# A hybrid decoder step on Trainium2: the activation region starts at a multiple of 256 bytes of SBUF

## The chip, the core and the metric

The kernel runs on one core of one Trainium2 chip. The core has TensorE (PE: matmuls, and PEld: its weight loads), VectorE (DVE), ScalarE (ACT), GpSimd (POOL), SyncE (SP), which here only issues DMAs, and 16 DMA engines. SBUF is the on-chip memory: 128 partitions, and every tensor has the same address in each. PSUM, in 8 banks, takes what TensorE computes. The metric is the time of one execution on the device in microseconds. The median of three runs of the kernel before is 1775.49 us.

## The reference

One step of a two-layer decoder for 288 tokens: a prompt of 256 and 8 samples of 4. All arithmetic is float32. Each layer has a mixer (a gated delta rule and a convolution module side by side) and a feed-forward part, which is dense in the first layer and has 8 experts, two for each token, in the second:

```python
for layer in range(DEPTH):
    mod = (jax.nn.silu(c) @ w_ada[layer] + b_ada[layer])[:, None, :]
    shift1, scale1, gate1, shift2, scale2, gate2 = jnp.split(mod, N_MOD, axis=-1)
    h = rms_norm(x, g_norm1[layer]) * (1 + scale1) + shift1
    proj = h @ w_in[layer]
    ...
    o_a, buf_a, s_a = gdn_mixer(qkv_in, z, b_raw, a_raw, ...)
    o_b, buf_b = conformer_conv(glu_u, glu_g, ...)
    x = x + gate1 * (jnp.concatenate([o_a, o_b], axis=-1) @ w_out[layer])
    h = rms_norm(x, g_norm2[layer]) * (1 + scale2) + shift2
    if layer % 2 == 0:
        f = swiglu(h, w_ff_gate[idx], w_ff_up[idx], w_ff_down[idx])
    else:
        f = moe_swiglu(h, w_router[idx], b_router[idx], w_exp_gate[idx], w_exp_up[idx], w_exp_down[idx])
    x = x + gate2 * f
return rms_norm(x, g_final), new_s, new_conv, new_conf
```

The model width is 1024, the dense hidden width 2816, that of an expert 3584. The outputs are the normed tokens and the new states of the delta rule and of the two convolutions.

## The kernel before

**Weights.** The host cuts all weights into units of 128 x 2048 float32 (1024 KB). SyncE loads 455 of them, one after the other, into a ring of six buffers, `raw`. Where precision asks for it, ScalarE rounds a unit to a high part in a ring of three, `whi` (line 666), and VectorE subtracts to get the low part in `wlo` (line 1040). TensorE then multiplies three times: high by high, high by low, low by high. These lines are 1681 to 1683 for tiles of weights against 288 tokens, and 2222 to 2224 in the expert stage.

**Stages.** First the modulation from the conditioning vectors (line 1692) and the first norm. Then, for each layer, the input projection, the mixer and the output projection, and the feed-forward part. In the dense layer the activations are the moving operand: eight tiles of `h_hi` and `h_lo` for the up projection (a loop of six units a turn), 22 tiles of `act_hi` and `act_lo` for the down projection. In the expert stage the roles are reversed: rows of gathered tokens (`ht_hi`, `ht_lo`) and of hidden values (`at_hi`, `at_lo`) are the stationary operand, and 512 columns of `whi` or `wlo` move. It is a loop over the experts' 42 units each, with the gather for the next expert and the scatter of the last one (`facc`, line 1599) put in between.

**SBUF.** The program lays its tensors out by hand. One big tensor, the arena, begins at 4224 and ends at 229304. Inside it `keep` hands out places in order: the three rings (12 buffers of 8192 bytes, the first at 4224), then `x`, the parameters, the constants and small tiles that live throughout. Where these end, at 139648, begins a region of 89088 bytes in which all else has its place as a fixed distance from the variable `r0`. Tiles of different stages share bytes there. The addresses of the rings are 128 above a multiple of 256, all of them, since 8192 is a multiple and 4224 = 16 x 256 + 128. So is 139648 = 545 x 256 + 128.

**What lies in the region**, with the distance from one tile to the next:

- 1152 bytes (288 tokens), so that tiles are in turn at 128 and 0 above a multiple of 256: `h_hi`, `h_lo`, `hf`, `sq`, `qkv`, `zs`, `yc`, `oall`, `act_hi`, `act_lo`, `facc`.
- a multiple of 256, so that all tiles lie as the region does: `ht_hi`, `ht_lo`, `at_hi`, `at_lo`, `ye_hi`, `ye_lo`, `pe_sel`, the 512-byte and 2048-byte blocks of the delta rule, the states `sst` (rows of 4096 bytes).
- neither: `qpad` (1260 bytes) and `cpad` (2232 bytes), the padded inputs of the two convolutions. VectorE reads them with a start that moves by 4 bytes for each tap (lines 1130 and 1110).

GpSimd issues the DMAs of the states and the pads: `sst<-gdn_in`, `gdns_out<-sst`, `qpad<-qst_in`, `cpad<-cst_in` and the outputs `qst_out` and `cst_out`. SyncE issues `y_out<-hf` at the end. No other DMA touches the region but that of the conditioning vectors at the start.

The order of work on every engine is written out in the program, and semaphores join the engines. No address has a part in it.

## Time and profile before

| | |
|---|---|
| median of 3 runs | 1775.49 us (1774.6 to 1776.69) |
| the profiled execution | 1778.42 us, its span 1776.6 us |
| TensorE busy | 1730.5 us, 97% |
| VectorE busy | 1370.4 us, 77% |
| ScalarE busy | 1034.5 us, 58% |
| GpSimd busy | 81.3 us, 5% |
| mean granted clock of TensorE | 0.976 of full speed |
| mean DMA rate | 281 GB/s |

The span goes from the first to the last instruction of the program; the execution's time is 1.8 us more. Busy times of engines overlap each other, so they say which engine has room, not which one sets the end. For that the profile follows a chain back from the last instruction, at each step to what released it. A matmul's recorded duration (390 ns for 512 columns) is longer than the distance of one from the next (227 ns), because they are pipelined: the starts of neighbours give the rate.

### The profile page before, as it was taken

What the parts mean: (1) busy time and instruction counts of PE and PEld (TensorE: products, weight loads), DVE (VectorE), ACT (ScalarE), POOL (GpSimd) and SP (SyncE); (2) the same over time, 40 slices, a digit from 0 to 9 for tenths busy, and PEclk for the clock granted to TensorE, in tenths of its full rate; (3) what the DMA queues carried; (4) which work ended last, traced back from release to release, by engine and by line L of the source; (5) the groups of instructions that cost most, each with busy time, mean ns of one, the idle gap of its engine ahead of it and who ended that gap; (6) DMA issues with size and microseconds to landing.
All of it is one profiled execution on the core that took longest, in us unless ns stands there. A gap on an engine that the chain in (4) does not pass through costs nothing.

```text
span 1776.6 us, 25456 instructions
## 1 busy us (share of the span) xinstructions
PE 1730.5 (97%) x9464; PEld 1448.7 (82%) x9464; DVE 1370.4 (77%) x1627; ACT 1034.5 (58%) x989; POOL 81.3 (5%) x97
## 2 busy tenths in 40 slices
PE   6999999999999999889999999999999999999997
PEld 3878977999978798668888888888888888888886
DVE  2698564554438984678898898898898988988998
ACT  3246423443333544157777777777777777777775
POOL 0112100000011220000000000000000000000000
PEclk8999899999999998989999999999999999999999
DMA  9686019444466520459999999999999999999996
GB/s 384 268 312 233 2 71 363 164 165 166 167 250 270 209 96 7 143 210 358 347 371 339 363 359 355 358 370 337 373 355 347 363 355 352 359 355 362 362 366 260
DMA packets 70186, 499.49 MB, mean 281 GB/s; under 512 B 7968, under 2 KB 8096, under 8 KB 11072
## 3 DMA queue, kind: packets, MB, share of 16 engines
q1 hardware_dynamic: 66528, 481.16, 71.2%
q0 software_dynamic: 3552, 16.87, 2.5%
q8 instruction: 72, 1.18, 0.3%
q14 instruction: 34, 0.28, 0.0%
HBM read 485.95 MB, written 12.05 MB: 280 GB/s over the span
## 4 chain that ended last, share of the span: by engine, by line
PE 91%; DVE 5%; DMA 2%; issue 1%; ACT 0%; SPq 0%; DVEq 0%
PE ps L2222 17%; PE ps L2223 17%; PE ps L2224 17%; PE ps L1681 5%; PE ps L1683 5%; PE ps L1682 5%; PE ps L2026 4%; PE ps L1863 3%; DMA raw<-units 2%; PE ps L1692 2%; PE ps L2199 1%; PE ps L2166 1%; PE ps L1702 1%; DVE yc L1110 1%; PE ps L1772 1%; PE ps L1787 1%
## 5 line engine op out<-in xcount | busy, mean ns | idle before, releaser
L1040 DVE TENSOR_TENSOR wlo<-raw,whi 128x2048 fp32r<-128x2048 f32 x384 | 876.8, 2292 | 180.3 <-ACT whi L666 180.3
L666 ACT ACTIVATE whi<-raw 128x2048 fp32r<-128x2048 f32 x384 | 735.9, 1918 | 251.5 <-PE ps L2224 203.1
L2222 PE MATMUL ps<-whi,ht_hi 128*128 128x512 f32 x896 | 355.5, 397 | 1.7 <-DVE ht_lo L1585 1.7
L2223 PE MATMUL ps<-wlo,ht_hi 128*128 128x512 f32 x896 | 349.4, 390 | 0.0
L2224 PE MATMUL ps<-whi,ht_lo 128*128 128x512 f32 x896 | 349.3, 390 | 0.0
L2224 PEld LDWEIGHTS ps<-whi,ht_lo 128*128 128x128 f32 x896 | 168.2, 188 | 35.9
L2222 PEld LDWEIGHTS ps<-whi,ht_hi 128*128 128x128 f32 x896 | 168.3, 188 | 34.9 <-issue 1.9
L2223 PEld LDWEIGHTS ps<-wlo,ht_hi 128*128 128x128 f32 x896 | 168.5, 188 | 31.4
L2222 PE MATMUL ps<-whi,at_hi 128*128 128x512 f32 x448 | 175.1, 391 | 0.0
L2223 PE MATMUL ps<-wlo,at_hi 128*128 128x512 f32 x448 | 174.4, 389 | 0.0
L2224 PE MATMUL ps<-whi,at_lo 128*128 128x512 f32 x448 | 174.4, 389 | 0.0
L1681 PE MATMUL ps<-h_hi,whi 128*128 128x288 f32 x560 | 167.6, 299 | 0.0
L1682 PE MATMUL ps<-h_lo,whi 128*128 128x288 f32 x560 | 165.5, 295 | 0.0
L1683 PE MATMUL ps<-h_hi,wlo 128*128 128x288 f32 x560 | 164.9, 294 | 0.0
L1681 PEld LDWEIGHTS ps<-h_hi,whi 128*128 128x128 f32 x560 | 105.3, 188 | 10.1 <-issue 8.4
L1683 PEld LDWEIGHTS ps<-h_hi,wlo 128*128 128x128 f32 x560 | 105.7, 189 | 0.0
L1682 PEld LDWEIGHTS ps<-h_lo,whi 128*128 128x128 f32 x560 | 105.5, 188 | 0.1
L1110 DVE SCALAR_TENSOR_TENSOR yc<-cpad,par,yc 128x256 f32<-128x256 f32 x240 | 104.2, 506 | 0.0
L2224 PEld LDWEIGHTS ps<-whi,at_lo 128*128 128x128 f32 x448 | 84.1, 188 | 17.6
L2222 PEld LDWEIGHTS ps<-whi,at_hi 128*128 128x128 f32 x448 | 84.1, 188 | 16.7
L2223 PEld LDWEIGHTS ps<-wlo,at_hi 128*128 128x128 f32 x448 | 84.1, 188 | 16.6
L2026 PE MATMUL ps<-hf,raw 128*128 128x288 f32 x352 | 91.7, 421 | 2.8 <-DVE hf L1090 2.8
(347 smaller groups left out, 2031.4 us busy)
## 6 DMA issues: line engine op xcount, KB each, us to landing
raw<-units SPq DMA_DIRECT2D x455, 1024.0 KB, 5.9
sst<-gdn_in POOLq DMA_DIRECT2D x8, 512.0 KB, 6.1
gdns_out<-sst POOLq DMA_DIRECT2D x8, 512.0 KB, 6.6
qst_out<-qpad POOLq DMA_DIRECT2D x2, 1890.0 KB, 9.0
cst_out<-cpad POOLq DMA_DIRECT2D x2, 1116.0 KB, 11.1
x<-x_in SPq DMA_DIRECT2D x1, 1152.0 KB, 9.1
y_out<-hf SPq DMA_DIRECT2D x2, 576.0 KB, 2.9
con<-const_in SPq DMA_DIRECT2D x1, 1141.5 KB, 18.8
```

The lines of the kernel that those rows point to most:

```text
L666: act.activation(whi[s % NSPLIT][:, :], raw[u % NRAW][:, :], ACT.Copy).then_inc(hi_split, 1)
L1040: dve.tensor_tensor(wlo[s % NSPLIT][:, :], raw[unit_of(s) % NRAW][:, :], whi[s % NSPLIT][:, :].bitcast(F32), ALU.subtract).then_inc(lo_spl ...
L1110: dve.scalar_tensor_tensor(y, cp3[:, c, j:j + TP], w, y, ALU.mult, ALU.add).then_inc(tap_prompt, 1)
L1681: mm(out, w_hi, x_hi, start=start, stop=False)
L1682: mm(out, w_hi, x_lo, start=False, stop=False)
L1683: return mm(out, w_lo, x_hi, start=False, stop=stop)
L1692: last = mm(ps[32 * k:32 * k + 32, bank, :], cst3[:, 4 * half + k], raw[u % NRAW][:, k * 512:(k + 1) * 512], start=(half == 0), stop=(half ...
L1863: last = mm(ps[:, bank, 0:T], raw[u % NRAW][:, w], part, start=(k == 0), stop=(k == 3))
L2026: last = mm(ps[:, bank, 0:T], raw[u % NRAW][:, w], hf3[:, k], start=(k == 0), stop=(k == KD - 1))
L2222: mm(ps[:, bank, :], a_hi[:, a], whi[u % NSPLIT][:, w], start=(first and i == 0), stop=False)
L2223: mm(ps[:, bank, :], a_hi[:, a], wlo[u % NSPLIT][:, w], start=False, stop=False)
L2224: last = mm(ps[:, bank, :], a_lo[:, a], whi[u % NSPLIT][:, w], start=False, stop=(end and i == 3))
```

## The change

The start of the region is rounded up to the next multiple of 256:

```diff
@@ -286,7 +286,7 @@
         posT = keep("posT", T)
         npass_i = keep("npass_i", 1, I32)
 
-        r0 = cursor[0]
+        r0 = (cursor[0] + 255) // 256 * 256
         h_hi = at("h_hi", r0, KD * T, F32R)
         h_lo = at("h_lo", r0 + 9216, KD * T, F32R)
         hf = at("hf", r0 + 18432, KD * T)
```

In the built program `r0` goes from 139648 to 139776 = 546 x 256. The 97 tensors of the region lie 128 bytes higher, and the other ones, with the rings at 128 above a multiple, stay. The region then ends at 228864, 440 bytes below the arena's end. On all five engines the instructions are the same ones in the same order.

The lines of the layout that the sections below speak of:

Of the kernel before, what the change touches and what calls it, by code (L numbers as in the profile page):

```python
# [254 lines left out]
def program(nc, units, x_in, c_in, par_in, const_in, gdn_in, qst_in, cst_in,  # L255
            y_out, gdnp_out, gdns_out, qst_out, cst_out):
    ctx = ExitStack()
    with ctx:
# [3 lines left out]
        cursor = [base]  # L262

        def at(name, offset, cols, dt=F32):
            return nc.alloc_sbuf_tensor_at(name, [P, cols], dt, offset=offset)
# [20 lines left out]
        posT = keep("posT", T)  # L286
        npass_i = keep("npass_i", 1, I32)

        r0 = cursor[0]
        h_hi = at("h_hi", r0, KD * T, F32R)  # L290
        h_lo = at("h_lo", r0 + 9216, KD * T, F32R)
        hf = at("hf", r0 + 18432, KD * T)
# [2072 lines left out]
```

## Rows read from the trace of the kernel before

**Rows 1.** The page: busy times (share of the span), and the chain by engine.

```profile
PE 1730.5 (97%) x9464; PEld 1448.7 (82%) x9464; DVE 1370.4 (77%) x1627; ACT 1034.5 (58%) x989; POOL 81.3 (5%) x97
...
PE 91%; DVE 5%; DMA 2%; issue 1%; ACT 0%; SPq 0%; DVEq 0%
```

**Rows 2.** By stretch: length, busy PE, PEld, DVE, ACT, POOL; clock, DMA share, GB/s.

```profile
298.00:411.00 113.00, 113.00 (x849) 113.00 (x849) 56.50 (x54) 53.27 (x58) 0.00 (x0) 1.00 0.50 179
830.00:1570.00 740.00, 740.00 (x3414) 613.66 (x3413) 658.57 (x443) 542.28 (x372) 0.00 (x0) 1.00 0.94 357
```

**Rows 3.** Waits, 765 to 1756 us: waiter, waited for, us in total, times, longest.

```profile
ACT whi L666 <- PE ps L2224: 202.3, 255, 2.2
```

**Rows 4.** VectorE alone in a stretch: length, busy (instructions), clock, DMA share, GB/s.

```profile
567.50:613.80 46.30, 44.54 (x95) 1.00 0.57 223
```

**Rows 5.** The chain in order of time, two pieces: start, length, what.

```profile
270.94 11.56 DMA raw<-units
...
510.42 6.71 DMA raw<-units
```

**Rows 6.** TensorE in the up loop: start, length, instruction.

```profile
329.82 0.30 PE L1681 MATMUL ps<-h_hi,whi 128*128 128x288 f32 x1
...
330.22 0.29 PE L1681 MATMUL ps<-h_hi,whi 128*128 128x288 f32 x1
...
330.62 0.30 PE L1681 MATMUL ps<-h_hi,whi 128*128 128x288 f32 x1
```

**Rows 7.** TensorE in the down projection.

```profile
440.46 0.30 PE L1681 MATMUL ps<-act_hi,whi 128*128 128x288 f32 x1
...
440.86 0.29 PE L1681 MATMUL ps<-act_hi,whi 128*128 128x288 f32 x1
```

**Rows 8.** TensorE in the expert stage; eight matmuls stand between these.

```profile
911.16 0.39 PE L2223 MATMUL ps<-wlo,ht_hi 128*128 128x512 f32 x1
...
913.20 0.39 PE L2223 MATMUL ps<-wlo,ht_hi 128*128 128x512 f32 x1
```

**Rows 9.** The page's groups of instructions: count, busy us, mean ns, idle before.

```profile
L1040 DVE TENSOR_TENSOR wlo<-raw,whi 128x2048 fp32r<-128x2048 f32 x384 | 876.8, 2292 | 180.3 <-ACT whi L666 180.3
...
L2222 PEld LDWEIGHTS ps<-whi,ht_hi 128*128 128x128 f32 x896 | 168.3, 188 | 34.9 <-issue 1.9
...
L2222 PEld LDWEIGHTS ps<-whi,at_hi 128*128 128x128 f32 x448 | 84.1, 188 | 16.7
```

**Rows 10.** Weight loads of `hf` at line 2003: one stretch, then all.

```profile
64.42 2.76 PEld L2003 LDWEIGHTS ps<-par,hf 128*128 128x128 f32 x24
...
L2003 PEld LDWEIGHTS ps<-par,hf x96: 106/192/192, 63.5 to 544.6; 128*128 128x128 f32 x64, 128*32 128x32 f32 x32
```

**Rows 11.** Lines with tiles 1152 bytes apart: minimum, median, maximum in ns.

```profile
L1599 DVE TENSOR_TENSOR facc<-ps,facc x56: 448/449/451, 907.0 to 1689.5; 128x288 f32<-128x288 f32 x56
...
L1468 DVE TENSOR_TENSOR act_lo<-ctmp,act_hi x22: 457/458/460, 299.2 to 433.5; 128x288 f32 x18, 128x288 fp32r<-128x288 f32 x4
...
L964 ACT ACTIVATE act_hi<-ctmp x22: 442/444/445, 298.6 to 433.0; 128x288 f32 x18, 128x288 fp32r<-128x288 f32 x4
```

**Rows 12.** The taps of the two convolutions, the same view.

```profile
L1110 DVE SCALAR_TENSOR_TENSOR yc<-cpad,par,yc x240: 469/477/1316, 61.0 to 653.7; 128x256 f32<-128x256 f32 x120
...
L1130 DVE SCALAR_TENSOR_TENSOR conv<-qpad,par,conv x36: 529/536/975, 107.2 to 614.7; 128x312 f32<-128x312 f32 x36
```

**Rows 13.** The page's DMA issues: count, KB each, median us to landing.

```profile
sst<-gdn_in POOLq DMA_DIRECT2D x8, 512.0 KB, 6.1
gdns_out<-sst POOLq DMA_DIRECT2D x8, 512.0 KB, 6.6
...
y_out<-hf SPq DMA_DIRECT2D x2, 576.0 KB, 2.9
```

**Rows 14.** GpSimd's DMA issues in order of time.

```profile
263.31 0.55 POOL L642 DMA_DIRECT2D gdns_out<-sst  x1 [26.80 <-DVE sst L1410]
...
506.28 1.06 POOL L605 DMA_DIRECT2D qpad<-qst_in  x1 [0.43 <-issue]
```

## The prediction, made before the changed kernel ran

> **What bounds the kernel now.** I read the page first, then the chain of waits, then stretches of the trace. TensorE is busy for 1730.5 us, 97% of the span of 1776.6, and the chain of work that ended last is 91% TensorE and 5% VectorE, with 2% of DMA [rows 1]. So there are three places in which an address could cost time. Most of it is matmuls back to back: in the expert stage from 830 to 1570 us TensorE is busy all the time at full granted clock, while ScalarE and VectorE have slack and the DMA engines are 94% busy; the loop of the dense layer's up projection (298 to 411 us) is TensorE alone too [rows 2]. The waits of the expert stage agree: ScalarE's `whi` waits 202.3 us for TensorE [rows 3]. VectorE sets the pace in one stretch, the second layer's input projection from 567.5 to 613.8 us, where it is busy for 44.5 us of 46.3 [rows 4]. DMA is waited for on the chain at 270.9 us (11.56 us) and at 510.4 us (6.71 us), both times for weight units; these are the pieces with transfers of the region near them [rows 5].
>
> **The change, part by part.** The change adds no instruction and no wait, and takes none away: all engines' orders are the same. What it does is raise 97 tensors by 128 bytes. Before, the region begins at 139648, which is 128 above a multiple of 256; after, at 139776, which is such a multiple. The rings stay at 128 above one. I call what is left over by 256 the phase. So every term is one question: what does phase 0 instead of 128 cost or save for each kind of access? The trace of before answers most of it, because many tiles of the region are 1152 bytes apart, four and a half times 256: every second one is at phase 0 already, and after the change they only swap.
>
> *Moving operands of TensorE.* In the up loop three matmuls in a row read tile k of `h_hi` and `h_lo`, the next three tile k+1 at the other phase, all against weights at phase 128. The first of three starts at 329.82, 330.22 and 330.62 us: 0.40 us for three at either phase [rows 6]. The same holds for `act_hi` and `act_lo` in the down projection (440.46 to 440.86 us) [rows 7]. The 1680 matmuls on `h_hi` and `h_lo` and the 528 on `act_hi` and `act_lo` swap phases among themselves and cost 0.
>
> *Stationary operands of TensorE.* In the expert stage the region holds the stationary side (`ht_hi`, `at_hi`, their low parts), 3 x 896 + 3 x 448 = 4032 loads at phase 128 before and 0 after [rows 9], and the ring the moving side at 128, unchanged. Nine matmuls go by from 911.16 to 913.20 us, 227 ns each, and a weight load takes 188 ns beside them [rows 8, 9]. A load at phase 0 is seen where the 64 wide loads of `hf` for the gates run: tiles k and k+1 at the two phases, 24 loads in 2.76 us, 115 ns each, with a median and a maximum that are both 192 ns [rows 10]. Were tiles at one phase slower, the two could not be the same. A load can thus follow another after 115 ns, against a spacing of 227 ns in the expert stage: it would have to take 112 ns more to be seen at all. Cost 0; cover 4032 x 227 ns of matmuls.
>
> *ScalarE and VectorE.* The 384 splits of weights read and write rings only and keep their addresses. Operations on tiles that alternate between the phases show one duration: `facc` 448 to 451 ns over 56, `act_lo` 457 to 460 over 22, `act_hi` 442 to 445 over 22 [rows 11]. Where tiles are not a whole number of 128 bytes apart, `yc<-cpad` reads at 31 steps of 4 bytes with 469 to 477 ns from minimum to median, and the taps of `qpad` 529 to 537 [rows 12]: a spread of up to 8 ns, under 2%, whose cause the trace does not show. The maxima of 1316 and 975 ns are far outside of such a spread, and as the order of the engines' work stays, I leave them where they are. GpSimd itself has no part of the chain [rows 1]. If this spread came from addresses, the shift could take or give 8 ns for each of the operations on the path. In the VectorE stretch there are 95 operations [rows 4]: 95 x 8 ns = 0.76 us. Outside of it VectorE holds about 5% of 1776.6 less 44.5 us, some 44 us [rows 1], much of it of the kinds that show one duration; 1% of that is 0.4 us. I take 0 and keep -1.2 and +1.2 us for the range.
>
> *DMA.* Weight units land in the rings and don't change. Into and out of the region go small transfers. `sst<-gdn_in` writes it in 6.1 us and `gdns_out<-sst` reads it in 6.6 us, for the same 512 KB and both at phase 128 [rows 13]. The two differ by 0.5 us, 8%, and that is the most that I can charge to the phase when a transfer reads the region. On the path it could act twice: four `gdns_out` issues, the first at 263.3 us, stand beside the weight units that TensorE waits 11.56 us for [rows 5, 14], at most 8% of 11.56 = 0.9 us; and the last `y_out` of 2.9 us, 0.2 us [rows 13]. Each could be a gain of 0 to 1.1 us together. As a loss I allow the same 8% on writes: `qpad` and `cpad`, issued from 506.3 us on [rows 14], share the DMA engines with the weight units that TensorE awaits for 6.71 us from 510.4 us [rows 5]: 0.5 us. The writes of `sst` are issued well before their values are read and are in no piece of the chain above. Between 0.5 and -1.1 us I take 0, because the two transfers that differ by 8% are both at phase 128, so what sets them apart is not the phase.
>
> The Trainium skill has a rule for this part (DMA: Bandwidth & Descriptors, section How a descriptor splits into AXI transactions): a descriptor that doesn't start at a multiple of 256 bytes begins its first transaction at the boundary below, and the bytes before its start cost beats. By it a row of 4096 bytes at phase 128 costs 132 beats instead of 128, and the reads out of the region would get 3% cheaper: an estimate of 3% of 11.56 + 2.9 us = 0.4 us, and a sum of 1775.1 us. The trace neither confirms nor excludes 3%: the reading transfer is the slower one by 8%, but it also runs beside weight units.
>
> *Sum.* 0 + 0 + 0 + 0, with bounds from -1.2 - 1.1 = -2.3 us to +1.2 + 0.5 = +1.7 us. The profiled execution took 1778.4 us with a span of 1776.6, 1.8 us outside of it; the sum is made against the span and carries over to the median of 1775.5, as the 1.8 us (start and end) touch no address of the region in another way. Predicted: 1775.5 us.
>
> **Rivals.** *Slower: crossed phases.* Before, stationary and moving operands of the expert stage are both at phase 128; after, one is at 0 and the other at 128. If two reads of TensorE at different phases got into each other's way, each of 4032 matmuls would pay. From 0.88 ns each (3.55 us, 0.2% of 1775.5) it shows; at one clock of 2.4 GHz, 0.42 ns, it is 1.7 us and hidden in the noise, at ten, 4.2 ns, it is 16.8 us and gives 1792 us. Against it speaks the up loop, where phases are crossed for every second tile at no cost [rows 6]; for it, only that there the roles are reversed and that this pairing of the expert stage is nowhere in the trace. Chance 6%.
>
> *Faster: the region's accesses were paying for phase 128.* Then the 14 ns between 227 ns and the 213 ns that 512 columns take at 2.4 GHz [rows 8] would be in part a penalty for the load from the region. If 1 ns of the 14 went, 4032 x 1 ns = 4.0 us, 1771.5 us; if all went, 56 us. Against it: the up loop has 133.3 ns for 288 columns, which are 120 ns: the same 13 ns, with its weights from the ring, and at both phases of the activations [rows 6]. The same 13 ns where nothing but the reader's side is exchanged is the mark of a fixed cost of a matmul. The gain from transfers alone (1.1 us) stays below what counts. Chance 6%.
>
> *The change does not do what it says.* The allocation could have put the region at a multiple already, or the rounding could push the last tensor out of the arena. Neither is so: 139648 is 545.5 x 256, and the region's end, 89088 above its start, lies 440 bytes below the limit. The result would be 1775.5 us all the same.
>
> **How the numbers follow.** A measurement of this kernel can tell 0.2%, 3.55 us, from no change; its three runs lie within 2.1 us. No change to be seen: 88% (the last rival is in it), 1775.5 us. Slower by crossed phases 6%, faster 6%. The range that holds 8 in 10 takes the bounds of the sum, -2.3 and +1.7 us, and 1.2 us of spread of the median on either side: 1772.0 to 1778.4, rounded to 1772.0 to 1778.5 us. It leaves both 6% out.
>
> **What would show it.** In the profile after, the starts of three matmuls in the up loop stay 0.40 us apart, and those of the expert stage 0.227 us; a step wrong there would be the whole result. The busy time of `wlo`, 876.8 us, stays within 1 us [rows 9]. `yc<-cpad` keeps its median of 477 ns; if it moves by several ns, the spread did come from addresses. `gdns_out<-sst` at 6.1 instead of 6.6 us would say that reads out of the region paid for their phase. The prediction is wrong if any matmul group's mean spacing changes by a ns, or if TensorE gets new waits of several us.

## The result: 1.1% slower, and all of it in the expert stage

The changed kernel takes 1793.14 us, the median of four runs (1790.23 to 1799.02). The kernel before took 1774.60, 1776.69 and 1775.49 us beside it; a fourth run of it took 1931.77 us, 9% more, which counts as a slow run, and all comparisons go by fast ones. The ratio of the two is 1.0113, with a 95% interval from 1.0085 to 1.014; the medians differ by 17.7 us, where no change was predicted. The profiled execution of the changed kernel took 1793.16 us with a span of 1791.4.

The page of the changed kernel, busy times, the chain by engine, and the groups that answer to [rows 1, 3, 9] (busy us, mean ns, idle before):

```profile
PE 1744.7 (97%) x9464; PEld 1445.5 (81%) x9464; DVE 1372.5 (77%) x1627; ACT 1033.8 (58%) x989; POOL 76.9 (4%) x97
...
PE 91%; DVE 5%; DMA 2%; issue 1%; ACT 0%; SPq 0%; DVEq 0%
...
L1040 DVE TENSOR_TENSOR wlo<-raw,whi 128x2048 fp32r<-128x2048 f32 x384 | 878.2, 2291 | 206.1 <-ACT whi L666 205.8
L666 ACT ACTIVATE whi<-raw 128x2048 fp32r<-128x2048 f32 x384 | 735.5, 1917 | 275.7 <-PE ps L2224 218.3
```

TensorE is busy for 14.2 us more with the same 9464 matmuls. VectorE and ScalarE do the same work in the same time; what grew is what they wait. In the expert stage ScalarE's `whi` waits for TensorE for 218.3 us instead of 202.3 [rows 3]. The chain has the same shares as before. So this is no new wait and no new bound: the engine that was the bound has become slower.

The same stretches as in [rows 2], in the changed kernel (length; busy PE, PEld, DVE, ACT, POOL with their numbers of instructions; clock, DMA share, GB/s):

```profile
830.00:1570.00 740.00, 740.00 (x3341) 601.45 (x3340) 646.97 (x431) 531.19 (x364) 0.00 (x0) 1.00 0.92 349
298.00:411.00 113.00, 113.00 (x849) 113.00 (x849) 57.12 (x53) 52.83 (x57) 0.00 (x0) 1.00 0.46 165
```

Both stretches are wholly TensorE's, at full granted clock, before and after, so the count in the bracket stands for its rate. In the up loop it is 849 matmuls before and after. In the expert stage it is 3341 instead of 3414: the same 3414 would now take 740 x 3414 / 3341 = 756.2 us, 16.2 us more in three quarters of the stage.

Single matmuls show it too. The changed kernel's expert stage (start, length, instruction):

```profile
911.20 0.39 PE L2223 MATMUL ps<-wlo,ht_hi 128*128 128x512 f32 x1
...
911.67 0.39 PE L2222 MATMUL ps<-whi,ht_hi 128*128 128x512 f32 x1
911.89 0.40 PE L2223 MATMUL ps<-wlo,ht_hi 128*128 128x512 f32 x1
912.13 0.39 PE L2224 MATMUL ps<-whi,ht_lo 128*128 128x512 f32 x1
912.36 0.40 PE L2222 MATMUL ps<-whi,ht_hi 128*128 128x512 f32 x1
...
913.29 0.40 PE L2223 MATMUL ps<-wlo,ht_hi 128*128 128x512 f32 x1
```

Nine intervals from 911.20 to 913.29 us are 232 ns each, against 227 [rows 8]; and they are uneven, 0.22 and 0.24 us in turn. For the whole stage I take from the trace the distance from one start to the next wherever six matmuls of the stage stand in a row: 3327 intervals with a mean of 227.0 ns before, 3332 with 233.3 ns after, mostly as 229 and 237 or 238 in turn. Before, over nine in ten of them are 226 or 227 ns, 226.7 in the mean, and the rest are mostly 231 to 233. At 2.4 GHz, 0.4167 ns a clock, 226.7 ns are 512 + 32 clocks, and 233.3 ns are 512 + 48. So most intervals grew by 16 clocks, 6.7 ns, and the mean by 6.3 ns. I call this mean the expert interval below.

The weight loads of line 2222 on `ht_hi`, an answer on one line of the program (minimum, median, maximum in ns, then the two times), before and after:

```profile
L2222 PEld LDWEIGHTS ps<-whi,ht_hi x896: 186/188/192, 772.7 to 1746.8; 128*128 128x128 f32 x180
```

```profile
L2222 PEld LDWEIGHTS ps<-whi,ht_hi x896: 186/188/192, 766.6 to 1761.2; 128*128 128x128 f32 x180
```

From first to last it is 974.1 us before and 994.6 after, 20.5 us more. Taken from the first to the last matmul of the stage, it is 986.1 and 1006.9 us, 20.8 more. The account closes: 3330 intervals x 6.3 ns = 21.0 us. The other 560 or so from one expert matmul to the next, which stand just behind matmuls of another kind or are above 260 ns, have a mean of 242.6 ns before and 242.3 after; together they take no longer. The load itself has not become longer, 188 ns as before.

The span is 14.8 us longer and not 20.8, because the stage begins earlier: at 772.7 us in the execution profiled before, at 766.6 after. Over the kernels below, but for the one with 256 columns in the up loop, it begins between 762 and 773 us, at any phase. Of the 6.1 us, 4.3 are there already at the first matmul of line 1681, 48.6 us into the span before and 44.3 after. The phase of the region doesn't set that start: two kernels below with the region at 128 have it at 44.6 us (the region by 256) and at 48.5 us (rings at 0). One execution of each kernel is profiled, so how the 17.7 us between the medians are made up is not shown.

### The profile page after: what moved, and what is told of

It is laid out like the page before. It is cut to its first block, busy times and chain, and to the rows that moved or that the text cites. A ratio compares the mean times of both kernels' runs of the same rounds, so it can differ in the third digit from the quotient of the medians.

```text
span 1791.4 us, 25456 instructions
## 1 busy us (share of the span) xinstructions
PE 1744.7 (97%) x9464; PEld 1445.5 (81%) x9464; DVE 1372.5 (77%) x1627; ACT 1033.8 (58%) x989; POOL 76.9 (4%) x97
## 4 chain that ended last, share of the span: by engine, by line
PE 91%; DVE 5%; DMA 2%; issue 1%; ACT 0%; SPq 0%; DVEq 0%
PE ps L2224 17%; PE ps L2222 17%; PE ps L2223 17%; PE ps L1681 5%; PE ps L1683 5%; PE ps L1682 5%; PE ps L2026 4%; PE ps L1863 3%; DMA raw<-units 2%; PE ps L1692 2%; PE ps L2199 1%; PE ps L2166 1%; DVE yc L1110 1%; PE ps L1772 1%; PE ps L1787 1%; PE ps L1785 1%
## 5 line engine op out<-in xcount | busy, mean ns | idle before, releaser
L1040 DVE TENSOR_TENSOR wlo<-raw,whi 128x2048 fp32r<-128x2048 f32 x384 | 878.2, 2291 | 206.1 <-ACT whi L666 205.8
L666 ACT ACTIVATE whi<-raw 128x2048 fp32r<-128x2048 f32 x384 | 735.5, 1917 | 275.7 <-PE ps L2224 218.3
L2224 PE MATMUL ps<-whi,ht_lo 128*128 128x512 f32 x896 | 354.1, 395 | 0.0
L2223 PE MATMUL ps<-wlo,ht_hi 128*128 128x512 f32 x896 | 353.5, 395 | 0.0
```

What stands on the lines that cost most here:

```text
L666: act.activation(whi[s % NSPLIT][:, :], raw[u % NRAW][:, :], ACT.Copy).then_inc(hi_split, 1)
L1040: dve.tensor_tensor(wlo[s % NSPLIT][:, :], raw[unit_of(s) % NRAW][:, :], whi[s % NSPLIT][:, :].bitcast(F32), ALU.subtract).then_inc(lo_spl ...
L2223: mm(ps[:, bank, :], a_hi[:, a], wlo[u % NSPLIT][:, w], start=False, stop=False)
L2224: last = mm(ps[:, bank, :], a_lo[:, a], whi[u % NSPLIT][:, w], start=False, stop=(end and i == 3))
```

## Experiments

Phase, as in the prediction, is an address by 256; the difference is the phase of the region's tile less that of the ring's. All kernels are the kernel before with the edit shown, where nothing else is said. `r0` is where the region begins. Each table's time is the median with the number of its runs; the expert interval and those of the 288-column loops are means over the trace, from start to start.

### Is it the region's phase, or the two phases against each other?

Everything by 128 bytes, rings and region:

```diff
-        base = (nc.sbuf_base + 63) // 64 * 64
+        base = (nc.sbuf_base + 255) // 256 * 256
```

> Rings and region both at a multiple of 256 (phase 0): the arena starts 128 bytes higher than in the kernel before, the region stays directly behind the small tiles. Seen so far: with rings at 128 and region at 128 a matmul of the expert stage follows the last after 226.7 ns, with rings at 128 and region at 0 after 229 and 237.5 ns in turn, 233.3 on average. Theory 1, only the difference of the phases counts: 226.7 ns again, and a time of 1773 to 1778 us. Theory 2, a stationary operand at phase 0 is slow wherever the moving one lies: 233.3 ns and 1790 to 1796 us. The new DMA phase of the weight units: up to 1 us less by either.

The same, and the region another 128 bytes on, so that the rings (and the small tiles between them and the region) are at 0 and the region at 128:

```diff
-        base = (nc.sbuf_base + 63) // 64 * 64
+        base = (nc.sbuf_base + 255) // 256 * 256
...
-        r0 = cursor[0]
+        r0 = cursor[0] + 128
```

> The reverse of the change: rings at phase 0, region at phase 128. Theory 1 (the difference counts): crossed again, 233.3 ns in the expert stage and 1790 to 1796 us. Theory 2 (stationary operand at phase 0): 226.7 ns and 1773 to 1778 us. The up loop, whose stationary operands are now at phase 0: 0.40 us for three matmuls by theory 1, more than 0.40 by theory 2 if it holds for any stationary operand.

The region by 256 bytes, which changes its place but not its phase, and by 64:

```diff
-        r0 = cursor[0]
+        r0 = cursor[0] + 256
```

> Control: rings unchanged, the region 256 bytes higher, so at phase 128 as before. If only the address modulo 256 counts: 226.7 ns, the time of the kernel before within 0.2%, 1773 to 1778 us. If the distance or a larger power of two counts: something else, up to the 1793 us of the change.

> Rings unchanged at 128, the region 64 bytes higher than before, at phase 192: the phases differ by 64. If the cost grows step by step with the difference: about half of the change's, 230 ns and 1784 us. If any difference costs the same: 233.3 ns and 1793 us. If only a difference of 128 costs: 226.7 ns and 1776 us.

| | rings at | region at | time, us | ratio to before, 95% interval | expert interval |
|---|---|---|---|---|---|
| before (19 runs beside them) | 128 | 128 | 1772.30 | | 227.0 ns |
| all by 128 | 0 | 0 | 1772.98 (10) | 1.0006 (0.9987 to 1.0025) | 227.0 ns |
| region by 256 | 128 | 128 | 1772.43 (10) | 0.9989 (0.9969 to 1.0008) | 227.0 ns |
| all but the region by 128 | 0 | 128 | 1794.31 (4) | 1.0124 (1.0089 to 1.0159) | 233.3 ns |
| region by 64 | 128 | 192 | 1793.09 (4) | 1.0114 (1.0079 to 1.0149) | 233.3 ns |

The expert stage between 830 and 1570 us, of the kernel with all at 0, and of the one with all but the region at 0:

```profile
830.00:1570.00 740.00, 740.00 (x3413) 613.30 (x3412) 659.04 (x444) 542.67 (x372) 0.00 (x0) 1.00 0.94 357
```

```profile
830.00:1570.00 740.00, 740.00 (x3342) 601.47 (x3341) 646.83 (x431) 530.61 (x363) 0.00 (x0) 1.00 0.93 349
```

3413 and 3342 matmuls: the first is the kernel before (3414), the second the changed one (3341). So a region at a multiple of 256 is neither good nor bad, and nor is a ring. What counts is that both have the same phase. The row of the region by 256 speaks against a cause in some single place, such as a boundary that a tile comes to lie across.

A rival is that TensorE's reads collide with the accesses of others. The trace of the changed kernel answers it. In the expert stage there are 192 intervals in which VectorE is idle (and idle through the next matmul too), and their mean is 232.9 ns; in 406 ScalarE is idle, 234.2 ns; in 17 no DMA packet is under way, 233.8 ns. The same groups of the kernel before have 226.7 ns each (130, 371 and 13 intervals). So the cost is there when each of the others is silent: it is TensorE's own operands that get into each other's way.

### At which differences?

One run each, the edit being another number added to `r0`:

> Rings unchanged, region 32 bytes higher than before (phases differ by 32). The runs so far: a difference of 0 gives 227.0 ns a matmul in the expert stage, 64 and 128 give 233.3 ns. Theory A, any difference costs the 6.3 ns: 233.3 ns, 1790 to 1796 us. Theory B, the two reads of TensorE collide in pieces of 64 bytes, and a smaller shift leaves them in the same piece for half of the time: 227 to 233 ns, 1773 to 1790 us.

> Region 96 bytes higher (difference 96). Theory A: 233.3 ns in the expert stage. Theory B: between the 233.3 ns of 64 and of 128, so the same. For the loops with 288 columns: 133.3 ns at a difference of 0 and 128, 132.3 ns at 64; at 96 I expect one of these two.

> Region 160 bytes higher, the mirror of 96 (160 = 256 - 96). If only the distance of the phases counts: the numbers of the region at 96. If it matters which of the two is ahead: other numbers. Expert stage 233.3 ns by theory A.

> Region 192 bytes higher, the mirror of 64. If only the distance counts: 233.3 ns in the expert stage and 132.3 ns in the loops with 288 columns, 1793 us. If it matters which is ahead: other numbers.

> Region 224 bytes higher, the mirror of 32, which had 233.3 ns. If the cost falls towards 256 as it did at 192 (229.2 ns): 227 to 229 ns and about the time of the kernel before. If not: 233.3 ns.

| added to `r0` | 0 | 32 | 64 | 96 | 128 (the change) | 160 | 192 | 224 | 256 |
|---|---|---|---|---|---|---|---|---|---|
| expert interval, ns | 227.0 | 233.3 | 233.3 | 234.3 | 233.3 | 233.3 | 229.2 | 233.3 | 227.0 |
| interval of the up loop, ns | 133.3 | 133.3 | 132.2 | 132.2 | 133.3 | 133.3 | 132.2 | 132.2 | 133.3 |
| time, us | | 1799.32 | 1793.09 | 1797.48 | 1793.14 | 1794.66 | 1776.42 | 1792.80 | 1772.43 |

The kernel before ran once beside 32, 96, 160 and 192, with 1772.69 us, and once beside 224, with 1779.27. The expert stage with 192 added:

```profile
830.00:1570.00 740.00, 740.00 (x3385) 609.43 (x3384) 655.25 (x441) 538.04 (x370) 0.00 (x0) 1.00 0.94 354
```

In the expert stage it is a step, not a slope: nearly any difference costs the same, 96 one ns more, and 192 only 2.2 ns. I have no explanation for 192. In the up loop tiles are 1152 bytes apart, so a loop holds two differences, the number added and that plus 128. Values with the same two agree there: 0 with 128, 32 with 160, 64 with 192, 96 with 224.

### Only the expert stage?

All tiles of the expert stage are raised by 128 bytes, and the tiles of all other stages stay. Two of the 17 lines of the edit:

```diff
-        ht_hi = [at(f"ht_hi{i}", r0 + 70656 * i, D, F32R) for i in range(2)]
+        ht_hi = [at(f"ht_hi{i}", r0 + 128 + 70656 * i, D, F32R) for i in range(2)]
...
-        at_hi = [at(f"at_hi{i}", r0 + 16384 + 16128 * i, 512, F32R) for i in range(2)]
+        at_hi = [at(f"at_hi{i}", r0 + 128 + 16384 + 16128 * i, 512, F32R) for i in range(2)]
```

> Only the tiles of the expert stage lie 128 bytes higher, in otherwise the kernel before; the mixers' and the dense layer's tiles stay at their phase. If the change costs its time in the expert stage alone: 233.3 ns there and the change's 1790 to 1796 us. If part of it comes from elsewhere: less, down to 1776 us.

Measured: 1792.70 us (4 runs) beside 1775.67 (7), ratio 1.0122, interval 1.0066 to 1.0178; expert interval 233.3 ns. The stage takes 1007.0 us, as with the full change (1006.9). The same stretch and single matmuls of it:

```profile
830.00:1570.00 740.00, 740.00 (x3341) 601.38 (x3340) 646.91 (x431) 531.25 (x364) 0.00 (x0) 1.00 0.93 349
```

```profile
910.99 0.40 PE L2223 MATMUL ps<-wlo,ht_hi 128*128 128x512 f32 x1
911.23 0.39 PE L2224 MATMUL ps<-whi,ht_lo 128*128 128x512 f32 x1
911.46 0.40 PE L2222 MATMUL ps<-whi,ht_hi 128*128 128x512 f32 x1
```

That is the whole of the change's cost, as far as the runs can tell. The transfers and VectorE's and ScalarE's operations on the rest of the region are where they were in this kernel, so no share of it is seen there.

### Which operand?

Of three matmuls, the first streams `whi` against `ht_hi`, the second `wlo` against `ht_hi`, the third `whi` against `ht_lo`. In one kernel only the low stationary parts go to phase 0 (the tiles around them are moved by multiples of 256 to make room, but `sge` and `ae` by 128); in the other the ring `wlo` does, and with it `x`, the parameters and the small tiles behind it:

```diff
-        ht_lo = [at(f"ht_lo{i}", r0 + 70656 * i + 4096, D, F32R) for i in range(2)]
+        ht_lo = [at(f"ht_lo{i}", r0 + (70656 + 512) * i + 4096 + 128, D, F32R) for i in range(2)]
```

> In the kernel before, only the low parts of the stationary operands of the expert stage (one load in three) go to phase 0; moving operands and the high parts stay at 128. In a row the matmuls are hi with whi, hi with wlo, lo with whi. Theory 1a, a load collides with the matmul that runs while it goes on: the matmul before the low one, on wlo, has the longer interval. Theory 1b, it is the matmul that uses the operand: the low one's own interval grows. If the cost belongs to each crossed pair: on average a third of 6.3 ns, 229.1 ns, 1776 + 8 = 1784 us; if it comes from a change of phase from one load to the next, more than that.

```diff
+        cursor[0] += 128
         wlo = [keep(f"wlo{i}", UNIT, F32R) for i in range(NSPLIT)]
...
-        r0 = cursor[0]
+        r0 = cursor[0] + 128
```

> Kernel before, with the three buffers of wlo (and what is behind them up to the region) 128 bytes higher: of the three matmuls in a row of the expert stage only the middle one has its moving operand at phase 0, all else is at 128. If a matmul pays for its own pair or for the load beside it: only the middle one's interval is longer, 233, and the average 229.1 ns. If the one after it pays too, as in the run with the low parts at phase 0: two of three, 231.3 ns.

| interval that begins with | `whi`, hi | `wlo`, hi | `whi`, lo | time, us (1 run) |
|---|---|---|---|---|
| before | 226.8 | 227.0 | 227.0 | |
| changed | 233.2 | 233.4 | 233.2 | |
| low stationary parts at 0 | 227.5 | 232.4 | 233.8 | 1790.25 |
| `wlo` at 0 | 234.4 | 233.4 | 230.3 | 1795.43 |

The loads of the kernel with the low parts at 0 (start, length, instruction) say what runs beside what:

```profile
911.04 0.19 PEld L2224 LDWEIGHTS ps<-whi,ht_lo 128*128 128x128 f32 x1
```

```profile
911.04 0.40 PE L2223 MATMUL ps<-wlo,ht_hi 128*128 128x512 f32 x1
911.27 0.40 PE L2224 MATMUL ps<-whi,ht_lo 128*128 128x512 f32 x1
```

The weights of the next matmul are loaded while the present one streams. If each interval paid for the pair that runs in it, the low parts at 0 would lengthen only the interval of `wlo`, in which `ht_lo` is loaded. It does, to 232.4 ns; but the next one, in which `ht_hi` at 128 is loaded beside `whi` at 128, is 233.8 ns. With `wlo` at 0 all three are longer. Neither run gave the 229.1 ns of a cost for each crossed pair alone: the mean over the three is 231.3 ns with the low parts at 0 and 232.7 with `wlo` at 0. So one operand out of step costs more than its own interval, and which two of TensorE's accesses collide stays open.

### Does the cost go by columns or by matmuls?

The changed kernel with 480 columns, and with 288, in each matmul of the expert stage; the other 32 or 224 columns of each result are left out of the computation:

```diff
-                                w = slice(i * 512, (i + 1) * 512)
+                                w = slice(i * 512, i * 512 + 480)
```

> The changed kernel with 480 instead of 512 columns in the expert stage's matmuls (32 columns of each weight tile are left out). 480 columns are 7.5 times 256 bytes. Theory: the collision costs 16 clocks for each matmul, whatever its width: 480 + 48 clocks, 220.0 ns. Rival: it goes by how the row ends against 256, as with 288 columns, which are 4.5 times 256 and show no cost: 480 + 32 clocks, 213.3 ns.

> The changed kernel, with 288 of the 512 columns in each matmul of the expert stage (the other 224 columns of each result are left out of the computation). Theory A (a matmul whose moving operand lies in the ring and whose stationary one lies in the region pays about 16 clocks at any width): 288 + 48 clocks, 140.0 ns of a matmul. Theory B (narrow matmuls pay little, whichever operand is where, as the 288-column up loop does): 133.3 ns, the up loop's value. The stage may then wait for its transfers or evictions, so the interval is read inside a run of back-to-back matmuls; the time itself says little, some 1400 to 1500 us.

With 480 columns (1745.39 us, one run), most intervals have one value:

```profile
910.95 0.38 PE L2223 MATMUL ps<-wlo,at_hi 128*128 128x480 f32 x1
...
911.16 0.38 PE L2224 MATMUL ps<-whi,at_lo 128*128 128x480 f32 x1
...
912.90 0.38 PE L2223 MATMUL ps<-wlo,at_hi 128*128 128x480 f32 x1
```

From 910.95 to 912.90 us, nine intervals, they are 217 ns; but three quarters of the stage's intervals are 220 ns, 480 + 48 clocks, and the mean is 219.1 ns. So at 480 columns the usual excess over the columns is the same 48 clocks as at 512, and a row that ends in the middle of 256 bytes doesn't escape the cost. The run can't tell a cost for each matmul from one for each column: 16 x 480 / 512 are 15 clocks. Nor was a kernel with equal phases run at 480.

With 288 columns (1674.17 us, one run, far more than the 1400 to 1500 that I expected; the stage now waits in between, at 911.15 us 0.70 us for VectorE's `facc`) the second theory came true:

```profile
912.37 0.29 PE L2222 MATMUL ps<-whi,ht_hi 128*128 128x288 f32 x1
...
913.57 0.29 PE L2222 MATMUL ps<-whi,ht_hi 128*128 128x288 f32 x1
```

Nine intervals in 1.20 us are 133.3 ns, 288 + 32 clocks, and all of the stage's intervals below 150 ns have a mean of 133.4. That is just what the up loop takes, in which the roles are reversed. So with crossed phases it is the width and not the role of the operands that sets the interval. What equal phases would give in the expert stage at 288 columns was not run.

### Was the up loop a fair comparison?

The prediction read from [rows 6] that crossed phases cost nothing. In the up loop every second tile of `h_hi` and `h_lo` is crossed with the rings. In these two kernels the loop reads only the even tiles (all at phase 128, none crossed), or only the odd ones (all crossed). The other half of the activations is left out of the computation and the first half is used twice, or the reverse:

```diff
-... hi3[:, k], lo3[:, k],
+... hi3[:, k // 2 * 2], lo3[:, k // 2 * 2],
```

> Kernel before, but the up projection's matmuls read the even tiles only (tile 0, 0, 2, 2, ... instead of 0, 1, 2, 3, ...; the same number of matmuls, the products of the odd tiles are wrong), so that moving and stationary operands are all at phase 128. Theory C, tiles in turn at both phases pay on both sides alike, which hid the cost: with equal phases the interval falls from 133.3 ns to 288 + 16 clocks, 126.7 ns, or some other value under 133, and the time by up to 1056 x 6.7 ns = 7 us. Theory D, 288 columns don't pay at all: 133.3 ns.

> The same with the odd tiles only (1, 1, 3, 3, ...), so that moving operands are at phase 0 and stationary ones at 128, crossed throughout. Theory C: more than with the even tiles, 133.3 ns or up to 140. Theory D: 133.3 ns.

The stretch from 298 to 411 us, all TensorE, of the kernel with the even tiles, and of that with the odd ones:

```profile
298.00:411.00 113.00, 113.00 (x861) 113.00 (x859) 57.40 (x54) 53.27 (x58) 0.00 (x0) 1.00 0.45 167
```

```profile
298.00:411.00 113.00, 113.00 (x849) 113.00 (x849) 56.34 (x54) 53.27 (x58) 0.00 (x0) 1.00 0.46 168
```

With the even tiles there are 861 matmuls; with the odd ones 849, as in the kernel before [rows 2]. From start to start that is 131.7 ns, 288 + 28 clocks, against 133.3, 288 + 32. Both kernels use each tile twice, so only the phase sets them apart. A crossed 288-column matmul does cost 1.7 ns, 4 clocks, much less than the 6.7 ns that I had thought possible, and in the kernel before the tiles that aren't crossed pay as well, since each of them stands between crossed ones: both phases took 0.40 us for three because both were paying. The times, 1775.75 and 1768.91 us beside a single 1779.27, are one run each; the loop's gain of 1056 x 1.7 ns = 1.8 us would be lost in their scatter.

One more kernel asked whether the up loop's interval is set by its columns or by the weight loads beside it: 256 columns instead of 288, the 32 tokens of the samples being left out of the up projection.

> Kernel before, but in the dense layer's up projection the matmuls take 256 columns instead of 288 (the 32 tokens of the samples are left out there). Theory 3, the loops with 288 columns are bound by weight loads and so hide the collision: the interval stays 133.3 ns. Rival, they are bound by their columns like the expert stage: 256 + 32 clocks, 120.0 ns, and the time falls by 1056 x 13.3 ns = 14 us.

```profile
298.00:411.00 113.00, 113.00 (x962) 113.00 (x961) 63.77 (x61) 57.34 (x64) 0.00 (x0) 1.00 0.54 196
```

962 matmuls instead of 849, and 117.8 ns from start to start against 133.3. I had expected 120.0 from the columns; 117.8 are 256 and some 27 clocks. The interval falls with the columns, so the idea that the loads (187 ns recorded) set the pace in this loop, and hide a cost there, has fallen. The time was 1760.07 us (one run) beside 1775.67.

### A version with the better phase for each stage

In the table of differences the 288-column loops take 1 ns less with the region 64 bytes on, where only the expert stage loses. So: `r0` 64 bytes on, and the expert stage's tiles back at their old addresses.

```diff
-        r0 = cursor[0]
+        r0 = cursor[0] + 64
...
-        ht_hi = [at(f"ht_hi{i}", r0 + 70656 * i, D, F32R) for i in range(2)]
+        ht_hi = [at(f"ht_hi{i}", r0 - 64 + 70656 * i, D, F32R) for i in range(2)]
```

> The region begins 64 bytes later than in the kernel before, and the tiles of the expert stage alone are put back to their old addresses. Theory (the cost goes by the difference between the addresses of ring and tile, stage by stage): the expert stage returns to 227.0 ns of a matmul, and the 288-column loops take the 132.2 ns that they took with the region 64 bytes on, not 133.3: some 2200 matmuls by 1.1 ns are 2.4 us less, 1773 to 1774 us beside 1776. Rival (the region's start sets it for the whole program): 233.3 ns and 1792 us, as with the whole region 64 bytes on.

Measured: 1772.72 us (12 runs) beside 1774.33 (17), ratio 0.9984, interval 0.9967 to 1.0001. The intervals are as expected, 227.0 ns in the expert stage and 132.2 in the two loops. The ratio's interval still holds no change, so a gain of 2.4 us is neither shown nor excluded, and this version can't be told from the kernel before. What it shows is again that each stage's interval follows its own tiles' addresses.

## Why the prediction was wrong

**What bounds the kernel** was read rightly: a cost of TensorE in the expert stage went to the end in full: 21.0 us by count, 20.8 us in the length of the stage.

**Moving operands, 0:** right for this change, for a reason that I did not see. The up loop takes 133.3 ns before and after, and the down loop too. But my reading, that phases don't matter there, was wrong: without a crossed tile it would have been 131.7, as the kernel with the even tiles shows for the up loop.

**Stationary operands, 0:** this is the step that failed. It asked whether a load at phase 0 is slow by itself, and [rows 10] answered that rightly: the expert stage with all at phase 0 has 227.0 ns, and the recorded load stays at 188 ns. It then added that a load would have to take 112 ns more to be seen at all. That takes a load that overlaps a matmul to be free as long as it ends in time. The runs show that it isn't: the interval grew by 6.3 ns while the load's duration stayed the same, and it grew as well when only the low parts were moved, which TensorE reads in loads alone. The term is 3330 x 6.3 ns = 21 us, not 0.

**The rival of crossed phases** had the mechanism, its place and its point of decision, and its example (ten clocks, 1792 us) came close to the 1793.14 that was measured. That is luck: ten clocks were an example and no estimate, and 4032 x 4.2 ns happens to lie near 3330 x 6.3 ns. Its chance of 6% was far too small. I called the up loop evidence against it, with one loose end, that the roles are reversed. The loose end that mattered was another: 288 columns against 512. And "the same interval at both phases" in a loop in which phases take turns compares each matmul with its neighbours, not with a loop in which none is crossed. The pairing of the expert stage stood nowhere in the trace, so its cost was unknown, and a price in clocks for each of 4032 matmuls on the path belonged into the range.

**The rival "faster"** took the 13 to 14 ns above the bare columns for a fixed cost of a matmul, since it was the same in both loops. It was the same by chance: 32 clocks are the value without a crossed tile at 512 columns, and the value with crossed tiles at 288.

**ScalarE and VectorE, 0:** right. `wlo` takes 2291 ns, against 2292; its busy time is 1.4 us more, where I had allowed 1. `facc`, `act_hi` and `act_lo` differ by at most 2 ns in their medians. The taps of the convolution, which I had named as a test, have a median of 478 ns instead of 477, and keep their mean (506 before):

```profile
L1110 DVE SCALAR_TENSOR_TENSOR yc<-cpad,par,yc 128x256 f32<-128x256 f32 x240 | 103.9, 505 | 0.0
```

**DMA, 0:** right within what can be told. The transfer out of the region became faster, 6.0 us instead of 6.6 [rows 13], which the prediction had named as the sign that reads out of the region had paid for their phase. It isn't one. The changed kernel, then the one with the region by 256 bytes (phase 128), then the one with only the expert stage moved (the states' tiles where they were, at 128), count, KB, median us:

```profile
sst<-gdn_in POOLq DMA_DIRECT2D x8, 512.0 KB, 6.2
gdns_out<-sst POOLq DMA_DIRECT2D x8, 512.0 KB, 6.0
```

```profile
sst<-gdn_in POOLq DMA_DIRECT2D x8, 512.0 KB, 6.3
gdns_out<-sst POOLq DMA_DIRECT2D x8, 512.0 KB, 6.8
```

```profile
sst<-gdn_in POOLq DMA_DIRECT2D x8, 512.0 KB, 6.3
gdns_out<-sst POOLq DMA_DIRECT2D x8, 512.0 KB, 6.8
```

These alone would fit a small gain for reads at phase 0. The pages of all the runs don't: the read took 6.0 to 6.8 us in the nine kernels with the region at 128 (6.0 in both that change only which tiles the up loop reads) and 6.0 to 6.5 in the four with it at 0. The write took 5.8 to 7.3 and 6.1 to 7.4 us. This scatter at one phase is as wide as the 0.5 us that the prediction charged to the phase; no experiment isolated the transfers. On the path no gain is seen: the piece of the chain in which TensorE waits for weight units beside these reads is 12.86 us long in the changed kernel, and 11.56 before [rows 5].

```profile
268.15 12.86 DMA raw<-units
```

**The range** was made of the bounds of small terms and scatter of the runs, 6.5 us wide. It left out the only term with 4032 pieces on the path. The scatter was taken too small besides, from three runs within 2.1 us: 17 later runs of the kernel before lie between 1768.42 and 1784.94 us.

## What to carry to other kernels

Where fp32r matmuls of some 500 columns each load new weights, give the stationary operand and the moving operand that streams beside its load the same address by 256 bytes; to round one of two regions up to a nice boundary can make things worse. Before an address is changed, list which pairs of operands change their difference, multiply a few clocks by the number of matmuls on the path, and keep that in the range unless a row shows that very pair at that very width. A loop in which good and bad cases take turns is no measurement of either: look for a stretch of one kind alone.

## What the runs showed of the hardware

- A 512-column fp32r matmul whose stationary and moving operands differ in their address by 256 starts 233.3 ns after the one before in the mean, against 227.0 ns without a difference; most intervals went from 512 + 32 to 512 + 48 clocks of 2.4 GHz. Seven differences were measured: 32, 64, 128, 160 and 224 cost that, 96 cost 7.3 ns, 192 only 2.2 ns. With both at 0, both at 128, and one of them 256 bytes on, there is no cost.
- At 480 columns the usual crossed interval is 480 + 48 clocks; at 288 it is 288 + 32 (133.3 ns) in either assignment of the operands, against 288 + 28 (131.7 ns) in the up loop with no crossed tile. How the cost grows from 288 to 512 was not measured.
- The recorded duration of the weight load doesn't show it: in the expert stage its median is 187 or 188 ns in all of these kernels but one, where it is 192 at line 2222 (low parts at 0). Only the distance between starts does.
- The cost is there while VectorE, ScalarE or the DMA engines are silent (232.9, 234.2 and 233.8 ns), so it lies between TensorE's own accesses.
- Open: which two of them collide. Moving one operand of three out of step lengthened two or three of the three intervals.
